# Two transformer blocks on one core: the mixer's last rounds in a written-out order, and another order of up weights in both joints

## The reference

```python
att = _neighbourhood_attention(q, k, v, kc, vc, na_rpb[l], rows)   # 8 heads of 64, context of 256 tokens
sg = _spatial_gating(z[..., o1:o1 + SG_W], z[..., o1 + SG_W:o2], ...)
cv = _conformer_conv(...)            # depthwise conv, group norm, silu
y = concatenate([att, sg, cv]) @ w_out
x = x + mod_l[2] * y                 # gate from the modulation, c @ ada_w
h2 = _modulate(_rmsnorm(x, norm2_g[l]), mod_l[3], mod_l[4])
x = x + mod_l[5] * _conv_ffn(h2, ffn_w_up[l], ...)
...
h = rms_norm(x, norm_ffn_pre[l])     # second block
u = causal_dwconv(h @ w_up[l], conv_ffn_w[l])
f = (gelu(g) * a) @ w_down[l]
```

## Time and profile before

| | us |
|---|---|
| median of 3 runs | 1409.32 (1408.08 to 1411.05) |
| the profiled execution's own time | 1408.85 |
| its span | 1407.6 |
| TensorE busy | 1362.3 (97%) |
| VectorE busy | 759.6 (54%) |
| ScalarE busy | 604.2 (43%) |

### The profile page before, as it was taken

How to read it: one execution, slowest core, us unless ns; L and a number is a source line. 1 busy time by engine, 2 the same in 40 slices (tenths; PEclk the granted TensorE clock), 3 DMA queues, 4 the chain that set the end, 5 groups by cost and what they waited for, 6 DMA issues and landing times.

```text
span 1407.6 us, 17413 instructions
## 1 busy us (share of the span) xinstructions
PE 1362.3 (97%) x7040; PEld 1125.4 (80%) x7040; DVE 759.6 (54%) x1082; ACT 604.2 (43%) x866; POOL 7.0 (0%) x15
## 2 busy tenths in 40 slices
PE   5999998989999999999999999999999999999997
PEld 4777876878888888888888888788997888888886
DVE  4678865575555443335524444345767665663224
ACT  5646866453333333223334545334624443443221
POOL 0000000000000000000000000000000000000000
PEclk9999999999999999999999999999999999999999
DMA  9743321323432323323232121234402233223331
GB/s 379 279 132 138 130 72 57 129 77 135 148 135 90 104 86 98 95 83 104 69 111 70 65 75 45 76 93 140 142 1 88 93 96 108 96 86 98 95 95 60
DMA packets 43102, 150.45 MB, mean 107 GB/s; under 512 B 4752, under 2 KB 6928, under 8 KB 41872
## 3 DMA queue, kind: packets, MB, share of 16 engines
q1 hardware_dynamic: 42144, 144.76, 30.7%
q0 software_dynamic: 880, 4.59, 1.0%
HBM read 146.45 MB, written 2.10 MB: 106 GB/s over the span
## 4 chain that ended last, share of the span: by engine, by line
PE 86%; DVE 7%; ACT 3%; issue 2%; DMA 1%; SPq 0%; DVEq 0%; ACTq 0%
PE banks L580 26%; PE banks L582 25%; PE banks L581 25%; ACT w_hi L1317 1%; DVE w_lo L1866 1%; PE banks L721 1%; PE banks L724 1%; PE banks L732 1%; PE banks L1127 1%; PE banks L1126 1%; PE banks L865 1%; PE banks L1118 1%; PE banks L1154 1%; PE banks L694 1%; PE banks L848 1%
## 5 line engine op out<-in xcount | busy, mean ns | idle before, releaser
L580 PE MATMUL banks<-h_lo,w_hi 128*128 128x512 f32 (+1 forms) x1248 | 473.4, 379 | 7.9 <-DVE h_lo L2205 3.3
L582 PE MATMUL banks<-h_hi,w_hi 128*128 128x512 f32 (+1 forms) x1248 | 470.4, 377 | 0.0
L581 PE MATMUL banks<-h_hi,w_lo 128*128 128x512 f32 (+1 forms) x1248 | 469.8, 376 | 0.0
L1866 DVE TENSOR_TENSOR w_lo<-raw_w,w_hi 128x1024 fp32r<-128x1024 f32 (+2 forms) x221 | 256.2, 1161 | 322.3 <-ACT w_hi L1317 320.0
L1317 ACT ACTIVATE w_hi<-raw_w 128x1024 fp32r<-128x1024 f32 (+2 forms) x221 | 221.5, 1004 | 236.1 <-PE banks L582 211.0
L580 PEld LDWEIGHTS banks<-h_lo,w_hi 128*128 128x128 f32 x1248 | 234.8, 188 | 59.9 <-issue 8.3
L581 PEld LDWEIGHTS banks<-h_hi,w_lo 128*128 128x128 f32 x1248 | 235.0, 188 | 43.4
L582 PEld LDWEIGHTS banks<-h_hi,w_hi 128*128 128x128 f32 x1248 | 234.9, 188 | 42.3
L582 PE MATMUL banks<-a_hi,w_hi 128*128 128x512 f32 (+1 forms) x396 | 146.2, 369 | 0.0
L581 PE MATMUL banks<-a_hi,w_lo 128*128 128x512 f32 (+1 forms) x396 | 145.8, 368 | 0.0
L580 PE MATMUL banks<-a_lo,w_hi 128*128 128x512 f32 (+1 forms) x396 | 145.6, 368 | 0.0
(11 more groups left out here) (315 smaller groups left out, 1518.2 us busy)
## 6 DMA issues: line engine op xcount, KB each, us to landing
raw_w<-in_w_ffn_up SPq DMA_DIRECT2D x44, 512.0 KB, 3.6
raw_w<-in_w_up SPq DMA_DIRECT2D x44, 512.0 KB, 3.3
raw_w<-in_ada_rows SPq DMA_DIRECT2D x24, 512.0 KB, 4.0
early<-in_ada_turned SPq DMA_DIRECT2D x8, 1024.0 KB, 16.9
raw_w<-in_w_gates SPq DMA_DIRECT2D x16, 512.0 KB, 3.2
raw_w<-in_w_ffn_down SPq DMA_DIRECT2D x16, 448.0 KB, 3.3
raw_w<-in_w_down SPq DMA_DIRECT2D x16, 448.0 KB, 3.3
raw_w<-in_w_conv SPq DMA_DIRECT2D x12, 512.0 KB, 3.2
```

Of the source, the lines that this page charges most:

```text
L580: e.matmul(dst, lhs_hi, rhs_lo, start=first, stop=False)
L581: e.matmul(dst, lhs_lo, rhs_hi, start=False, stop=False)
L582: return e.matmul(dst, lhs_hi, rhs_hi, start=False, stop=last)
L1866: e.tensor_tensor(lo[:, 0:n], raw[:, i % RAW, 0:n], hi[:, 0:n].bitcast(F32), ALU.subtract).then_inc(s_lo, 1)
```

## The change

Out2's split moves from q3's end behind `gated1` on ScalarE, and q3's `after_tile` behind `mixed5` on VectorE. Two preloads of the Exp table are added. In the first joint `prepare` of the third up tile goes ahead of the first `second_hi` and the Silu table behind the half's last one; in the second FFN three up tiles are split one by one and earlier. Nothing of what is computed changes. The diff, cut to its core:

```diff
@@ mixer_order: the rounds after the twelfth are written out
     pairs = AC * CBLK
-    for i in range(pairs + 2):
...
+    ahead = pairs - CBLK
+    for i in range(ahead):
+        fill_until(f"q{i // CBLK}")
+        if i:
+            order.append(("factors", i - 1))
+        order.append(("scores", i))
+        if i == 0:
+            order.append(("exps", 0))
         fill_to(i, 0.55)
+        if i:
+            order += [("exps", i), ("turn", i - 1)]
         fill_to(i, 1.0)
         if i >= 2:
-            order.append(("values", i - 2))
-    return order
+            order += [("values", i - 2), ("attended", i - 2)]
...
+    last_chunk = KC - 1
+    order += own(len([step for step in left if step[0] not in ("out", "group_spread")]) - 3)
+    order += [("factors", ahead - 1), *own(3), ("turn", ahead - 1), ("scores", ahead), ("mixed", 0), ("mixed", 1), ("exps", ahead)]
+    order += [*spreads(), ("mixed", 2), ("mixed", 3), ("values", ahead - 2), ("attended", ahead - 2), ("values", ahead - 1)]
+    order += [*out(0, 0, 4), ("factors", ahead), ("gated", 0), ("scores", ahead + 1), ("turn", ahead), ("gated", 1), *out(1, 0, 4)]
+    order += [("mixed", 4), ("mixed", 5), ("attended", ahead - 1), ("exps", ahead + 1), *out(0, 4, last_chunk)]
+    order += [("values", ahead), ("attended", ahead), *out(1, 4, last_chunk)]
+    order += [("factors", ahead + 1), ("scores", ahead + 2), ("turn", ahead + 1), *out(2, 0, 4), ("exps", ahead + 2)]
+    order += [*out(2, 4, last_chunk), ("values", ahead + 1), ("attended", ahead + 1)]
+    order += [("factors", ahead + 2), ("scores", ahead + 3), ("turn", ahead + 2), *out(3, 0, 4), ("exps", ahead + 3)]
+    order += [*out(3, 4, last_chunk), ("values", ahead + 2), ("attended", ahead + 2), *out(4, 0, 4), ("factors", ahead + 3)]
+    return order + [("turn", ahead + 3), *out(4, 4, last_chunk), ("values", ahead + 3), ("attended", ahead + 3)]
@@ ScalarE, mixer
+                if group != "q3":
                     prepare(t + 4)
...
-                    if (group, last) == ("q3", True):
...
+                elif kind == "mixed" and of[0] < 4:
...
+                    split_hi(mixed_input(n), h_hi[:, OUT_ORDER[n], :], s_mix_hi)
+                    if n == 1:
+                        e.preload_act_table(ACT.Exp)
...
+                elif kind == "gated":
...
                     split_hi(cv_acc[:, c, :], h_hi[:, AC + SC + c, :], s_mix_hi)
+                    if c == CC - 1:
+                        e.preload_act_table(ACT.Exp)
+                        prepare(W["q3"] + 4)
@@ ScalarE, joint to the first FFN
             x1_square(KC, 2 * OUT_SPLIT + 4, x[:, LAST_TWO[0], HALVES[1]], squares[:, 1, HALVES[1]])
+            prepare(W["up"] + 3)
             e.wait_ge(s_mod, 2)
...
             second_root(1)
-            e.preload_act_table(ACT.Silu)
-            prepare(W["up"] + 3)
             for k in range(6, KC):
                 second_hi(0, k)
+            e.preload_act_table(ACT.Silu)
@@ ScalarE, second FFN
-                prepare(W["up2"] + ((7, 9)[f] if f < 2 else 2 * f + 4))
+                prepare(W["up2"] + ((7, 9, 10)[f] if f < 3 else 2 * f + 4))
...
                 split_hi(u, a2_hi[:, f, :], s_a2_hi.sem)
+                if 2 <= f < 4:
+                    prepare(W["up2"] + f + 9)
@@ VectorE, mixer
                 if kind == "scores":
-                    if of[0] >= 1:
-                        weight_factors(of[0] - 1)
-                    softmax(of[0])
...
+                    softmax(*of)
+                elif kind == "factors":
+                    weight_factors(*of)
+                elif kind == "mixed":
+                    n, = of
+                    mixed_lo(n, mixed_input(n))
+                    if n == 5:
+                        after_tile(W["q3"])
+                elif kind == "attended":
+                    attended_lo(*of)
...
-                    if last and (kind == "context" or group[0] != "k"):
+                    if last and group != "q3" and (kind == "context" or group[0] != "k"):
                         after_tile(t)
@@ VectorE, both joints
-            low(W["up"] + 3)
             second_lo(0, KC - 1)
+            low(W["up"] + 3)
...
-                low(W["up2"] + (2 * f + 6 if f else 9))
+                low(W["up2"] + (f + 9 if f < 3 else 2 * f + 6))
```

More of the change, by code:

```diff
@@ L234, in mixer_order @@
     pairs = AC * CBLK
-    for i in range(pairs + 2):
-        if i < pairs:
-            fill_until(f"q{i // CBLK}")
-            order.append(("scores", i))
+    ahead = pairs - CBLK
[6 more added lines that the diff above has]
+            order.append(("exps", 0))
         fill_to(i, 0.55)
-        if 1 <= i <= pairs:
-            order.append(("turn", i - 1))
+        if i:
+            order += [("exps", i), ("turn", i - 1)]
@@ L242, in mixer_order, with own, spreads, out @@
         fill_to(i, 1.0)
         if i >= 2:
-            order.append(("values", i - 2))
-    return order
+            order += [("values", i - 2), ("attended", i - 2)]
+    left = [step for _, step in fill[at:]]
+    def own(n):
+        taken = [step for step in left if step[0] not in ("out", "group_spread")][:n]
+        for step in taken:
+            left.remove(step)
+        return taken
+    def spreads():
+        return [step for step in left if step[0] == "group_spread"]
+    def out(o, first, beyond):
+        return [step for step in left if step[0] == "out" and step[1] == o and first <= step[3] < beyond]
@@ L387, in two_blocks, with mixed_input @@
         all_, tri, hidden, same = (minus[:, n * P:(n + 1) * P] for n in range(4))
+        def mixed_input(n):
+            return (q_loc, sg_out, cv_acc)[n // 2][:, n % 2, :]
         def x_normed(k):
@@ L1491, in scalar_program @@
             for kind, *of in MIXER:
[L1492 to L1496, removed]
-                elif kind == "turn":
[L1498 to L1504, removed]
+                if kind == "factors":
+                    normalised(*of)
+                elif kind == "exps":
+                    exponents(*of)
+                elif kind == "turn":
+                    copy_over(*of)
+                elif kind == "attended":
+                    attended(*of)
                 elif kind == "product":
@@ L1510, in scalar_program @@
                         gate_root()
-                    if (group, last) == ("q3", True):
[L1512 to L1517, removed]
+                elif kind == "mixed" and of[0] < 4:
+                    n, = of
+                    if n < 2:
+                        e.wait_ge(s_att, n + 1)
+                    else:
+                        e.wait_ge(s_sg_done, n - 1)
+                    split_hi(mixed_input(n), h_hi[:, OUT_ORDER[n], :], s_mix_hi)
+                    if n == 1:
+                        e.preload_act_table(ACT.Exp)
                 elif kind == "context":
@@ L2142, in vector_program @@
                         modulation_ready(2, 1)
[L2143 to L2146, removed]
-                        mixed_lo(3, sg_out[:, 1, :])
                 elif kind == "sg_mix":
@@ L2247, in vector_program @@
                     second_factor(1)
+            second_lo(0, KC - 1)
             low(W["up"] + 3)
-            second_lo(0, KC - 1)
             for k in range(KC):
```

8 lines of the change are left out of this document (2 added, 6 removed).

## The result

| | before | after |
|---|---|---|
| median of 4 runs each, same chip, us | 1410.18 (1408.08 to 1411.19) | 1417.32 (1416.88 to 1417.90) |
| ratio | | 1.0051 [1.0039, 1.0062] |
| profiled execution, span | 1408.85, 1407.6 | 1417.90, 1416.6 |
| TensorE busy, page | 1362.3 | 1366.7 |

The change makes the kernel slower by 0.5%. In a later set of runs the same changed kernel took 1415.17 against 1410.65: 1.0038 [1.0024, 1.0052]. The two intervals overlap, and both lie clear of 1. The forecast was 1413.7.

What follows compares the result with a forecast made beforehand. TensorE was taken as the bound, with time to be had only from its waits and clock. Mixer +7.8, first joint -0.7 and second FFN -2.3 gave +4.8 on 1408.85, so 1413.7 us; range 1405.0 to 1418.5.

Steps and rivals of the forecast that it cites:

- the slower chain: Rival for the mixer: tile loads land in 4.4 us twice, plus a second low-clock stretch; 1417.5 us or over, chance 0.15.
- sign of being wrong: In the mixer: out3's load issued before 226, or turn 13 starting before 240, would show the forecast wrong.
- wait at out0.6: Mixer, out0's chunk 6: TensorE waits 3.7 us, to 231.8, for that chunk's low part; before it waited 0.5.
- turns 14, 15 wait: Mixer's last rounds, each serial behind an output's end: TensorE waits 2.2 us, then 1.1 us.
- The row behind q3: VectorE's modulation row after q3, held by ScalarE's late split of out2; ends 231.1, so out3's load moves from 216.21 to 231.2.
- Two links: Mixer: reciprocal 13 stands behind two load-to-row steps of the raw tile chain, 6.75 us each, from 231.2 to 244.7.
- The wait of 8.8: Mixer, turn 13: TensorE is through at 236.9 and waits 8.8 us until 245.7, with 2.0 us charged for the clock.
- Joints: First joint gains 0.7 us from an earlier VectorE chain; second FFN gains 2.3 us from weight tiles split earlier.
- The rival that ended faster: Mixer: out3's load does not wait, one link goes, turn 13 waits 2 at full clock; 1405 us, chance 0.15.
- The rival with only the joints and turn 11: Mixer rounds 13 to 15 cost what they did before, the wait at turn 11 is won; 1398.6 us, chance 0.04.
- three unknowns: Error sources: clock -2.0 to 0, landing of two loads -0.8 to +1.8, ScalarE's small steps 1.4 either way; sum +1.5 to +8.
- The third case: Rival for the mixer: slow landings twice and a second low-clock stretch on the path; 1417.5 us or over, chance 0.15.

Runs made afterwards that it cites:

- second trace: Profile of the changed kernel run once more, unaltered, in a later set; median 1415.17 us of 4 runs.
- the joints alone: The kernel before with only the diff of both joints, nothing of the mixer's; median 1408.38 us against 1411.01, ratio 0.9976.
- the early row: Changed kernel with out2's high part ahead of reciprocal 12 on ScalarE, its low part and q3's `after_tile` behind that reciprocal on VectorE; 1412.77 us.

## Why the prediction was right, point by point

The forecast of 1413.7 was +4.8 on the profiled execution before. The two comparisons give +7.1 and +4.5, and the medians 1417.32 and 1415.17: the second is in the band of 1413 to 1416.5 that had 0.50, the first lies between it and the 1417.5 of the slower chain. The sign and the mechanism held. Neither sign of being wrong came (a load ahead of 226, a turn 13 ahead of 240). The terms, against both traces of the changed kernel:

| term | forecast | first trace | second trace |
|---|---|---|---|
| turn 11 starts, no wait | 212.3 | 214.12 | 212.65 |
| out2's high part | 227.9 | 229.92 | 228.34 |
| out3's load | 231.2 | 233.17 | 231.59 |
| wait at out0.6 | 3.7 | 3.48 | 3.47 |
| reciprocal 13 | 244.7 | 246.47 | 244.34 |
| turn 13 | 245.7 | 247.53 | 245.40 |
| its wait | 8.8 | 6.77 | 6.29 |
| turns 14, 15 wait | 2.2, 1.1 | 2.44, 0.96 | 2.44, 0.97 |
| values 15 end | 272.6 | 275.4 | 273.0 |

**The row behind q3.** The walk of ScalarE by its row lengths held: from the end of turn 11's copy to out2's high part it gave 13.5 us (214.4 to 227.9), and the traces have 13.5 in both (216.39 to 229.92, 214.80 to 228.34). What is later is where it begins. The walk charged a table load its 1.28 us and nothing more. The Exp load at 217.44 and its first exponent in the changed kernel:

```profile
217.44 1.28 ACT L1551 ACT_TABLE_LOAD   x1
218.74 0.69 ACT L1467 ACTIVATE squares<-banks,soft 128x512 f32<-128x512 f32 x1
```

They are 0.02 apart, and the copy before the load ends at 217.43. The Trainium skill (ScalarE: Activation LUTs, What ACT_TABLE_LOAD costs) adds a drain of about 1.38 us to every switch to a different set, which for the three switches makes an estimate of 4 us of delay for out3's load; the trace doesn't agree with it.

**Two links.** From the issue of out3 to reciprocal 13 it was 13.3 us in the first trace and 12.75 in the second, where 2 x 6.75 = 13.5 was charged. The second trace's 0.75 less made up for its start being 0.4 late, so that turn 13 fits to 0.3 is in part luck. That this chain holds turn 13 was shown by taking the reciprocal out of it.

**The wait of 8.8 was 6.3 to 6.8**, without moving turn 13. TensorE came to it later than the forecast 236.9, at 240.8 and 239.1, since it had started late and since the clock was already at 0.50 behind the 3.48 (235 to 238); the prediction had put that loss under the next wait at 0, and there it lay.

**Joints.** The first gave -0.7 for -0.7, the second FFN -2.1 for -2.3 (-2.3 in the second trace); the joints alone gave -3.

**The rival that ended faster** needed a row some 6 us earlier than 231.1. The experiment with the early row has it 9 us earlier than the second trace and came to 1412.77, level with before and not to 1405 (with the joints' -3 in it), because turns 14 and 15 kept their waits and turn 13 most of its. The estimate that one link gone would leave turn 13 a wait of 2 is the step of the prediction that is wrong, in two places. A whole link of 6.75 doesn't go: the next one can't begin before out0's last product (230.69), and turn 13 comes 4.1 earlier. And TensorE gains from the earlier row too and comes 4.1 sooner, so the wait stays (6.32 against 6.29).

**The rival with only the joints and turn 11** stood at 1398.6. The experiment that comes nearest to it, turn 11's part with the old rounds, took 1405.47: the gain at turn 11 is real, but smaller waits of 5.4 us take most of its place.

**The bounds.** The three unknowns at their low ends give 4.8 - 2.0 - 0.8 - 1.4 = +0.6, not the +1.5 of the text; the high end is right.

**What was missed.** In both traces TensorE begins the last three products of q3 some 0.4 later (210.56 and 210.49, before 210.11). In the first trace alone there are about 1.4 of low clock at 211 to 214, where the prediction had expected full clock to 228, and 1.6 in the joint at 1020 to 1037. The third case, "a second low-clock stretch on the path", had named such a thing, but as a drop behind a wait.

## What to carry to other kernels

An engine takes its instructions in order, so ask of every small operation that another engine waits for (here a reciprocal of 0.16 us) what stands ahead of it and which transfer that hangs on; put it directly behind its input. When a step moves, follow what it sets free: behind a row of 1.2 us came a load, a high part, a low part and the next row, 6.4 us from one load to the next (233.17 to 239.61). Lead that TensorE wins early is kept only if the operands of the next stage come earlier too: of the 17 to 19 us won at the mixer's end 12 to 15 reached the end of the kernel, and a copy ahead of the first chunk of the joint was worth 1.4 to 1.9 of the rest. Compare two orders at a point that ends the same work in both: values 15 are the mixer's last step in one and stand three products ahead of it in the other.

## What the runs showed of the hardware

The lower clock level came in short stretches with TensorE busy in them and for at least 2 us ahead of them: 211 to 214 in one execution of the changed kernel and not in another, 1023 to 1027 in the first and 1037 to 1042 in the second, 1029 to 1033 in the kernel before. Each of these four begins within some 1 us of the end of a row of matmuls only one or two columns wide (16 of 128x2 from 208.75, sums of squares of 128x1 from 1020.98, 1033.84 and 1026.32). But the same rows also ran without a drop behind them (from 208.68 in the second trace, from 1011.36 in the kernel before), so they are not enough by themselves, and no run varied them.

The time of one kernel goes with its mean clock. Executions of the kernel before took 1410.2 to 1413.3 us at 0.988 and 1407.7 to 1409.4 at 0.993, in the mean 3.6 us for 0.005. The kernel without `after_tile` at out4's end took 1402.1 to 1403.5 at 0.990, and 1399.6 to 1401.2 at 0.993 and 0.994, in two sets of runs. So a comparison of a few executions of this kernel is uncertain by 2 us from that alone, and experiments are best read at like clock. Why a stretch comes in one execution and not in the next stays open.
